# Sixteen conditioning products as GpSimd-scaled slices: a two-block transformer kernel on one core

## The reference

```
for i in range(DEPTH):                                   # DEPTH = 2
    x = layer_norm(a * x + 0.5 * swiglu(x, ffn_w1[i, 0], ffn_w3[i, 0], ffn_w2[i, 0]), ...)
    mix = token_mixing(x, ...)
    x = layer_norm(a * x + mix, ...)
    x = layer_norm(a * x + 0.5 * swiglu(x, ffn_w1[i, 1], ffn_w3[i, 1], ffn_w2[i, 1]), ...)
    x = layer_norm(a * x + sigmoid(x @ ple_w_gate[i]) * (p[i] @ ple_w_proj[i]), ...)
```

```
mod_l = silu(c)     @ ada_w[i] + ada_b[i]     # shift, scale, gate of the latent stream
mod_c = silu(c_ctx) @ ada_w[i] + ada_b[i]     # the same of the context stream
```

## Time and profile before

| | |
|---|---|
| median of 3 runs | 3075.93 us (3074.19 to 3077.7) |
| span of the profiled execution | 3075.3 us |
| PE busy | 2984.1 us, 97% |
| DVE busy | 1734.7 us, 56% |
| ACT busy | 715.3 us, 23% |
| POOL busy | 77.7 us, 3% |
| granted TensorE clock, mean | 0.998 |

### The profile page before, as it was taken

The page is one execution under the profiler, slowest core; times in us unless marked ns, Lnnn a source line. Parts: engine busy times, 40 slices in busy tenths (PEclk is TensorE's granted clock), DMA queues, the critical chain, the costliest instruction groups (busy, mean ns, idle before and its releaser), DMA issues. The chain is left out here.

```text
span 3075.3 us, 53460 instructions
## 1 busy us (share of the span) xinstructions
PE 2984.1 (97%) x23086; PEld 2376.8 (77%) x23086; DVE 1734.7 (56%) x2567; ACT 715.3 (23%) x1371; POOL 77.7 (3%) x105
## 2 busy tenths in 40 slices
PE   8999999999999999999999999989999999999998
PEld 8988775559987998685558985655888887766897
DVE  5554456446556564464546556584333664486666
ACT  2102114222112101223322104282111012254210
POOL 1000000000001000000000000000000000001000
PEclk9999999999999999999999999999999999999999
DMA  8645403237656746313227744102222443231553
GB/s 288 223 175 184 142 30 110 97 110 234 206 183 196 260 164 216 134 60 108 99 83 234 237 141 151 55 1 83 82 82 83 150 154 113 98 122 63 165 165 110
DMA packets 279818, 429.94 MB, mean 140 GB/s; under 512 B 10072, under 2 KB 147776, under 8 KB 279584
## 3 DMA queue, kind: packets, MB, share of 16 engines
q1 hardware_dynamic: 273936, 411.52, 39.5%
q0 software_dynamic: 5024, 13.82, 1.4%
q10 hardware_dynamic: 624, 1.19, 0.1%
HBM read 425.45 MB, written 1.05 MB: 139 GB/s over the span
## 5 line engine op out<-in xcount | busy, mean ns | idle before, releaser
L460 PE MATMUL bank<-arena 64*64 64x64 f32 (+8 forms) x7292 | 740.9, 281 | 23.3 <-DVE arena L2069 4.6
L460 PE MATMUL bank<-xT,ring 128*128 128x128 f32 (+2 forms) x4512 | 725.1, 320 | 10.3 <-DVE arena L852 5.7
L460 PEld LDWEIGHTS bank<-arena 128*128 128x128 f32 (+3 forms) x7292 | 640.6, 161 | 120.1 <-issue 36.6
L460 PEld LDWEIGHTS bank<-xT,ring 128*128 128x128 f32 (+1 forms) x4512 | 657.7, 191 | 71.2 <-issue 10.5
L460 PE MATMUL bank<-ring,xT 128*128 128x512 f32 (+3 forms) x1648 | 577.2, 519 | 2.2 <-DVEq L2086 1.2
L460 PEld LDWEIGHTS bank<-ring,xT 128*128 128x128 f32 (+1 forms) x1648 | 264.0, 182 | 253.5 <-issue 237.0
L460 PE MATMUL bank<-ring,arena 128*128 128x256 f32 (+1 forms) x1584 | 436.9, 427 | 12.4 <-issue 5.3
L460 PEld LDWEIGHTS bank<-ring,arena 128*128 128x128 f32 x1584 | 298.2, 190 | 123.9 <-issue 82.0
L852 DVE TENSOR_TENSOR arena<-arena,bank 128x256 f32<-128x256 f32 (+1 forms) x198 | 92.2, 466 | 395.7 <-PE bank L460 254.7
L763 ACT COPY arena<-bank 128x256 f32<-128x256 f32 (+1 forms) x264 | 107.7, 408 | 747.2 <-PE bank L460 745.9
L812 DVE TENSOR_TENSOR arena<-ring,arena 128x1024 f32<-128x1024 f32 (+1 forms) x216 | 257.1, 1190 | 7.4
(11 more groups left out here) (421 smaller groups left out, 2186.8 us busy)
## 6 DMA issues: line engine op xcount, KB each, us to landing
ring<-in_ffn_w SPq DMA_DIRECT2D x88, 1024.0 KB, 8.0
ring<-in_w_in SPq DMA_DIRECT2D x32, 2048.0 KB, 7.7
ring<-in_ffn_w_in SPq DMA_DIRECT2D x44, 1024.0 KB, 6.5
arena<-in_ada_w SPq DMA_DIRECT2D x20, 2048.0 KB, 13.2
ring<-in_ffn_w SPq DMA_DIRECT2D x16, 2048.0 KB, 7.9
ring<-in_ffn_w_out SPq DMA_DIRECT2D x12, 2048.0 KB, 7.8
ring<-in_hgrn_w_in SPq DMA_DIRECT2D x12, 2048.0 KB, 7.9
ring<-in_ffn_w SPq DMA_DIRECT2D x8, 1536.0 KB, 6.6
```

The lines of the kernel that those rows point to most:

```text
L460: return self.e.matmul(o, lhsT, rhs, start=start, stop=stop, skip_group_check=True)
```

## The change

Sixteen of the 24 conditioning products are no longer made by 32 matmuls. GpSimd scales each of the 8 slices (128x512) of a block of ada_w by the vector's column for that slice (`tensor_scalar`, one scale for each partition) and adds the slices up (`tensor_tensor`); for the blocks that both streams need it does so twice. TensorE then only sums over the 128 partitions: 4 matmuls for each stream. Eleven of the sixteen need both streams (16 scalings and 14 additions), five only the latent one (8 and 7). All sixteen stand in the feed-forward networks, 3, 4, 4 and 5 of them, in FFN 3 one of these in the down part. The other eight remain products of 32 matmuls, come through the ring and stand in transitions: 3 and 2 in layer 0, 3 in layer 1.

`f_ada` is loaded in two halves of 1 MB, each with its own semaphores; a half is issued behind a ring block once GpSimd has done with the same half of the block before. The sums have two places (`ada_sum`), one in the arena and one in columns of xT. GpSimd's sums stand in its program ahead of, between and behind its DMA issues: in `pool_ada(f, after_first)` the DMA issues of the mixing stage (FFN 2) or the embedding (FFN 1 and 3) follow the first sum. Some semaphores are merged to make room.

```
         ada_rows = at(arena_cols - 4 * P, 4, P)
+        IN_DOWN = 12
-        IN_TRANSITION = ((2, 0, 1, 0), (2, 0, 0, 0))
-        IN_FFN = (((3, 5, 7, 8, 9), (3, 5, 7, 9)), ((3, 5, 7, 8, 9), (3, 5, 7, 8, 9)))
+        IN_FFN = (((5, 7, 9), (4, 6, 8, 9)), ((4, 6, 8, 9), (4, 6, 8, 10, IN_DOWN)))
+        TRANSITION = ((("ring",) * 3, (), ("ring",) * 2, ()), (("ring",) * 3, (), (), ()))
+        HOME_LOADS = ((2, 4, 6), (0, 2, 4, 6), (0, 2, 4, 6), (0, 2, 4, 6, 8))
...
+        def pool_ada(pool, f, after_first=None):
+            e = pool.e
+            pool.wait_ge(x_sums, x_sums_before(f) + 1)
+            first = sum(len(x) for x in HOME_LOADS[:f])
+            for i in range(first, first + len(HOME_LOADS[f])):
+                if i >= 2:
+                    pool.wait_ge(ada_used, i - 1)
+                streams = ada_streams(i)
+                for h in range(2):
+                    pool.wait_ge(ada_landed[h], pool.due(ada_landed[h], 16))
+                    for k in range(4 * h, 4 * h + 4):
+                        w_ = f_ada[:, k].rearrange("p (a b) -> p a b", a=2)
+                        scaled = []
+                        for s in streams:
+                            last = s == streams[-1]
+                            out_ = ada_sum(i, s) if k == 0 else w_ if last else ada_scaled
+                            if last and len(streams) == 2:
+                                pool.wait_ge(pool_step, scaled[0])
+                            e.tensor_scalar(out_, w_, c_wide[:, k, s:s + 1], None, ALU.mult).then_inc(pool_step, pool.up(pool_step))
+                            scaled.append(pool.sent(pool_step))
+                        for s in streams:
+                            if k:
+                                pool.wait_ge(pool_step, scaled[s])
+                                acc = ada_sum(i, s)
+                                e.tensor_tensor(acc, acc, w_ if s == streams[-1] else ada_scaled, ALU.add
+                                                ).then_inc(pool_step, pool.up(pool_step))
+                        if k:
+                            pool.wait_ge(pool_step, pool.sent(pool_step) - len(streams) + 1)
+                    pool.wait_ge(pool_step, pool.sent(pool_step))
+                    pool.sem_inc(ada_half_used[h], pool.up(ada_half_used[h]))
+                pool.sem_inc(ada_summed, pool.up(ada_summed))
+                if i == first and after_first:
+                    after_first()
...
             if home:
-                pe.wait_ge(ada_landed, pe.due(ada_landed, 16))
-                blk = f_ada
+                pe.wait_ge(ada_summed, pe.due(ada_summed))
+                pe.wait_ge(to_act.freed, to_act.next_free())
+                bank = to_act.free_bank()
+                streams = ada_streams(pe.homes)
+                for s in streams:
+                    for j in range(4):
+                        mm = pe.mm(bank[32 * j:32 * j + 32, 0:P], pick[:, 31 - s:63 - s],
+                                   ada_sum(pe.homes, s)[:, j // 2, j % 2 * P:j % 2 * P + P], s == 0, s == streams[-1])
+                mm.then_inc(to_act.filled, 1)
+                pe.homes += 1
+                return
...
+                def loaded():
+                    for h in range(2):
+                        if len(mine) - 1 - h in marks:
+                            modulation(h)
...
+            def modulation_half(h):
+                m = ADA_HOME[homes[h]]
+                if homes[h]:
+                    eng.wait_ge(ada_half_used[h], homes[h])
+                homes[h] += 1
+                eng.dma_start(f_ada[:, 4 * h:4 * h + 4], k_rows(a["ada_w_2"][m // 12], m % 12 * 512, 512)[:, 4 * h:4 * h + 4]
+                              ).then_inc(ada_landed[h], 16)
```

More of the change, by code:

```diff
@@ L144, in two_blocks @@
         ada_used = sem("ada_used")
-        ada_landed = sem("ada_landed")
+        ada_landed = [sem(f"ada_landed{h}") for h in range(2)]
+        ada_half_used = [sem(f"ada_half_used{h}") for h in range(2)]
+        ada_summed = sem("ada_summed")
         ada_rows_ready = sem("ada_rows_ready")
@@ L440, in first_loads @@
                 wide(a["w_o"][l], 0, 1024)
[L441 to L444, removed]
+                ffn(a["ffn_w1"][l, 1], 0, a["ffn_w3"][l, 1], 0, a["ffn_w2"][l, 1], modulation_half, HOME_LOADS[2 * l + 1])
+                modulation(TRANSITION[l][2].count("ring"))
                 load((None, 0, k_rows(a["ple_w_proj"][l], 0, 1024)))
                 wide(a["ple_w_gate"][l], 0, 1024)
-                modulation(IN_TRANSITION[l][3])
         class Tensor(Side):
@@ L1121, in act_transition @@
                 early()
[L1122 to L1125, removed]
+            products = TRANSITION[l][n]
+            for kind in products[:-1]:
+                act_ada_product(act, kind == "home")
+            act_ln_turn(act, l, n, 0, (0, 1), lambda: act_std(act, 1), len(products) > 0, products[-1:] == ("home",))
             if middle:
@@ L1145, in pe_transition @@
             pe_turn_x(pe, X2[1:], (to_act, to_dve))
-            for _ in range(products):
+            for _ in products:
                 pe_ada_turn(pe)
@@ L3029, in two_blocks @@
         ADA_BLOCKS = DEPTH * 6 * D // 512
[L3031 to L3038 removed]
+        ada_rows = at(arena_cols - 4 * P, 4, P)
@@ new lines, in two_blocks, with ada_streams, ada_sum @@
+        ADA_HOME = [n for n, kind in enumerate(ADA_KINDS) if kind == "home"]
+        ADA_RING = [n for n, kind in enumerate(ADA_KINDS) if kind == "ring"]
+        assert len(ADA_KINDS) == ADA_BLOCKS and len(ADA_HOME) == sum(len(x) for x in HOME_LOADS)
+        def ada_streams(i):
+            n = ADA_HOME[i]
+            return (0, 1) if n // 12 == 0 or n % 12 < 4 else (0,)
+        def ada_sum(i, s):
+            if i % 2:
+                return xT[:, 4 + 2 * s:6 + 2 * s, SEQ:512]
+            return f_ada_sum[:, s].rearrange("p (a b) -> p a b", a=2)
@@ L3052, in pe_ada_product @@
                                k == 0, k == KT - 1)
-                    if k == j == 0 and not home:
+                    if k == j == 0:
                         pe.release(mm)
@@ L4711, in ln, with mix_inputs @@
                     e.dma_start(lnp[:, j], w[l, n:n + 1, :].broadcast_to([P, D])).then_inc(ln_landed, 16)
-            for l in range(DEPTH):
+            def mix_inputs(l):
                 if l:
@@ L4716, in first_pool, with embedding_inputs @@
                 ln(l, 0)
-                pool_mix(pool, l)
+                pool_mix_rows(pool, l)
+            def embedding_inputs(l):
+                pool.wait_ge(ln_used, pool.due(ln_used))
+                ln(l, 2)
+                if l == DEPTH - 1:
+                    pool_second_inputs(pool)
+                pool_ple(pool, l)
+            for l in range(DEPTH):
+                if l == 0:
+                    mix_inputs(0)
+                pool_ada(pool, 2 * l, (lambda: mix_inputs(l)) if l else None)
+                pool_mix_lora(pool, l)
                 pool_gla(pool)
                 pool_gdn(pool)
-                for n in range(1, 4):
-                    if n > 1:
-                        pool.wait_ge(ln_used, pool.due(ln_used))
-                    ln(l, n)
-                    if n == 2:
-                        if l == DEPTH - 1:
-                            pool_second_inputs(pool)
-                        pool_ple(pool, l)
+                ln(l, 1)
+                pool_ada(pool, 2 * l + 1, lambda: embedding_inputs(l))
+                pool.wait_ge(ln_used, pool.due(ln_used))
+                ln(l, 3)
         @block.sync
```

118 lines of the change are left out of this document (57 added, 61 removed).

## The result

The changed kernel takes 3330.35 us (median of 4 runs, 3327.3 to 3331.22), the one before 3075.2 in the same session (4 runs): a ratio of 1.0825 [1.081, 1.0841], 8% slower. The forecast had the sign but 3190 us and an upper end of 3250. What follows finds the missing 140 us. The profiled execution has a span of 3328.1 us.

What follows compares the result with a forecast made beforehand. It took TensorE, busy for 97% of the span, as the bound: 3075.3 - 16 on TensorE (-29 and +13) + 132 of waiting for GpSimd = 3191, predicted as 3190 us. Likeliest case 3140 to 3250; 8 in 10, 3068 to 3250.

Steps and rivals of the forecast that it cites:

- TensorE -29: Up parts: nineteen products of 1.9 us leave (36 us), sixteen short ones come in (7 us), net -29 us.
- Transitions +13: Three transitions get one more ring product each: about 5.5 us twice before the mixing stage, about 2 before the embedding.
- GpSimd's time for a block, 27.4: Both streams: 14 additions at 1.0, 16 scalings at 0.75 and 8 waits at 0.17 us; ends 23.4 and 33.
- the forecast's own formula: FFN 1: four GpSimd blocks, 2 us of DMA issues and 46 of lost turns, less 111 until block 9, give 47.
- The turns lost, 46 us in FFN 1: VectorE's two-operand instructions set GpSimd back on the shared read interface, 4.35 to 4.75 us per block of TensorE.
- FFN 3, 3 us: One stream, about 16 us of GpSimd a block against 25 of TensorE, about even with turns lost: 3 us of waiting.
- Where the waits stand: Waits of some 130 us at block 9 and earlier, as VectorE waiting for blocks and TensorE for sums; none in down parts.
- A: Rival: GpSimd keeps up in the networks and all is hidden, 3059 us, faster; chance 15%.
- B: Rival: VectorE bears the whole collision, 15.7 instead of 12.6 us a block over 22 blocks, 3137 us; chance 20%.
- C: Rival: GpSimd late by little, transitions and waits take what TensorE saves, within 0.2% of 3076 us; chance 5%.

Runs made afterwards that it cites:

- TensorE makes all: The changed kernel without GpSimd's sums, all sixteen products made by TensorE with 32 matmuls each, halves of f_ada waiting for ScalarE's copy: 3092.51 us, ratio 1.0054.
- Few sums, far apart: The changed kernel with only two GpSimd sums in each of FFN 0 to 2, five conditioning blocks left out: 3096.28 us; with TensorE making the products instead, 3080.09.

## Why the prediction was wrong in size

**TensorE -29.** The short product was put at 0.5 us and measures 0.65 at full clock, 1.08 at half. Of no weight.

**Transitions +13: it was 20.6**, and 18.4 where TensorE makes all. The wait for the third ring place came as described, 4.99 us against the forecast's 3.3. From the first product to the mixing stage's first matmul with weights it was 10.3 us before and is 20.1 now, +9.8 where 5.5 was forecast. The third product starts 9.7 us after the first, not 8, and it and the turn behind it run at half clock, 2.5 us more. Some 2 us of the 9.8 come back in the mixing stage of layer 0.

**GpSimd's time for a block, 27.4: this is the step that failed.** The scaling was put between 0.5 and 1.1 us, "since one of two reads falls away". It measures 1.56. The one bound from above was a two-operand row, 1.1 us, and it was no bound. The addition's 1.0 came from line 2327; an addition in place measures 1.26. Whether that is the adding or the writing over an operand isn't separated. So a block is bare 42.6 us. With that, the forecast's own formula gives for FFN 1 4 x 42.6 + 2 + 46 - 111 = 107 us of waiting instead of 47, and for FFN 0 and 2 73 and 115 instead of 27 and 55: 298 with FFN 3's 3, and 3357 us in all. That is 29 us above the measured span, because the next term erred the other way.

**The turns lost, 46 us in FFN 1: too large.** Block 9's product starts 200 us after the first x sum (756.95 to 956.99). Less four bare blocks (170) and the DMA issues (2), 28 are left, in FFN 2 28 too, in FFN 0 20 instead of 33. The forecast made GpSimd lose nearly all of each meeting; in fact both lose. "Few sums, far apart" shows it where VectorE works at full pace: a block in FFN 1 takes 52.7 us, 10 more than bare, beside 4.2 of TensorE's blocks. That is 2.4 us for each of them, where the forecast had 4.35 to 4.75. VectorE's line 814 (128x1024) was to take 1.9 to 2.0 us in FFN 0 to 2 and takes about 1.5; no run brings it above 1.73 there. Over the whole run GpSimd's sums take 656 us (733.9 less the 77.5 of "TensorE makes all") where bare they would be 216 x 1.56 + 189 x 1.26 = 575, so it bears about 81 us. VectorE's line 814 takes 592 us in its three forms instead of 515, so it bears about 77. The Trainium skill (SBUF — State Buffer, "Who interferes with whom") has the one that holds the port block the other, whichever it is; the rows of 823 to 829 us agree, with 1.78 instead of 1.23 on VectorE and 2.25 and 2.53 instead of 1.26 and 1.56 on GpSimd. And while VectorE waits for a ring block that waits for GpSimd, GpSimd runs alone: a slow GpSimd meets VectorE less often, and its blocks take 48 to 50 us instead of 52.7. So counting the meetings from a VectorE at full pace added to the error.

**With the measured terms the sum closes.** This puts in the measured start of block 9's product, so it checks only that the time is lost ahead of it. FFN 1: 200 - 111 = 89 of waiting, less 5.6 of saved matmuls, is 83; measured 85.4. The rest is block 9's first 32 records, which take 6.14 us instead of 3.84, at half clock at first. FFN 2: 209 - 111 = 98, less 7.5, is 90.5; measured 91.9. FFN 0: the product starts at 187.3 instead of 129.4, so 58, less 8, is 50; measured 51.7. With FFN 3 and the transitions that is the whole 253.

**FFN 3, 3 us: right in size, partly by luck.** Bare, a block is 8 x 1.56 + 7 x 1.26 = 21.3 us there, not 16, and from end to end 26 to 29; the turns lost are fewer than forecast. The network measures 3.4 us more, made of two parts that the forecast didn't size: with memsets in place of the sums it is 7.6 under before, and the sums' reads put 11.0 on top. With one stream GpSimd's block is about as long as two of TensorE's (25.3), and TensorE is still busy at 9 tenths there.

**Where the waits stand: right.** Through the ring and VectorE, and at block 9. The fall of the clock in them wasn't foreseen. By the sums above it adds by itself only what is left after block 9's product, about 2 us a network; before it, the longer matmuls stand in stretches that GpSimd paces. No run holds the clock up in the networks, so that part is argued.

**Rivals.** A (GpSimd keeps up) had the slack worked out at GpSimd's price of 0.5 us, and failed with it. B (VectorE bears all) is half of the truth: it bears about half of the collision, and that cost 31 us where nobody waits for GpSimd, less than the 68 worked out; and it left out the pace. C (late by little) needed a bare pace near 25 us and fell with A. The range left the result out because its upper end rested on the 1.1 us.

## What to carry to other kernels

Before work goes to an idle engine, its pace decides: number of instructions times the measured price of just that form and operation, plus what it loses to a neighbour that reads beside it (10 us on 42.6 here), against the time until the first consumer. Where that price isn't in the trace, time it by itself first, and don't bound it by a form that looks more costly. A queue that is in order carries the wait on: here the weights of the main work stood behind an entry that waited for GpSimd, so its lateness appeared under the names of a DMA and of VectorE. And work in time isn't free: through VectorE it still cost 1 to 3 us for each network, net of the matmuls it saved.

## What the runs showed of the hardware

- On GpSimd, multiplying 128x512 float32 by one value for each partition took 1.56 us, by a broadcast column as second operand 1.04, and adding two in place 1.26. The Trainium skill (GPSIMD Engine Reference, "Engine selection") calls one-input operations "roughly line-rate". The trace disagrees for the scaling: 3.05 ns for each column, half as much again as the two-operand form, and the measurement decides.
- A GpSimd memset of 128x1600 took 1.43 us and left VectorE's two-operand subtractions at 1190 ns, their length when GpSimd does nothing.
- Where GpSimd's scalings and additions met VectorE's two-operand subtractions, an instruction of either took up to 1.1 us longer (2.67 instead of 1.56 and 2.25 instead of 1.26 on GpSimd, 2.20 instead of 1.23 on VectorE). The whole stream, 405 instructions that nobody waited for, cost the kernel 31 us.
- TensorE at a granted clock of 1.00 came back at 0.50 from a wait of 4.8 us, for a product of 3.64 us; with 40 matmul records of idle work in the gap it stayed at 1.00 and took 1.95.
